# Expert products of a hybrid decoder step: a store on another queue, another spread of row chunks, an earlier load

## The reference, cut to what matters

```
ue = u[e]
ve = v[e]
a = jax.nn.gelu(jnp.einsum('nd,nhkd->nhk', xb, ue, preferred_element_type=f32), approximate=False)
return jnp.einsum('nhk,nhkd->nd', (g * a).astype(x.dtype), ve).astype(x.dtype)
```

## Time and profile before

| | |
|---|---|
| median of 3 runs | 2511.35 us (2506.83 to 2520.95) |
| the profiled execution | 2510.1 us, its span 2508.5 us |
| u part, first product to last | 955.5 to 1691.8 us |
| v part, first product to last | 1709.3 to 2393.9 us |
| TensorE busy, share of the span | 87% |
| VectorE busy | 54% |
| ScalarE busy | 14% |
| moved by DMA | 511.81 MB, mean 204 GB/s |

### The profile page before, as it was taken

One profiled execution on the slowest core, in us unless ns is written; L12 is line 12 of the kernel. 1 busy time (PEld: TensorE's weight loads), 2 busy tenths in 40 slices (PEclk: granted clock), 3 DMA queues, 4 the chain that ended last, 5 costly groups with the idle time before them and its releaser, 6 DMA issues. The chain is left out here.

```text
span 2508.5 us, 24546 instructions
## 1 busy us (share of the span) xinstructions
PE 2177.9 (87%) x8879; PEld 1609.9 (64%) x8879; DVE 1360.6 (54%) x2817; ACT 358.3 (14%) x743; POOL 338.3 (13%) x316
## 2 busy tenths in 40 slices
PE   7968899869999899999987888887787788789997
PEld 4745687637889566777654666665555555457776
DVE  2006577644441796999854777774544555451022
ACT  1001276420101012111100122220000000000011
POOL 1011000030000002222222111112222222210000
PEclk9979999875599899999998999998989999889999
DMA  3241121131223326999888777769999999976521
GB/s 117 51 91 64 43 101 51 28 108 51 111 81 101 108 94 258 337 346 346 307 315 291 268 257 287 265 236 355 335 324 324 338 330 328 334 264 209 180 82 45
DMA packets 181423, 511.81 MB, mean 204 GB/s; under 512 B 16589, under 2 KB 103253, under 8 KB 154038
## 3 DMA queue, kind: packets, MB, share of 16 engines
q1 hardware_dynamic: 146358, 294.72, 35.1%
q0 software_dynamic: 31488, 213.94, 22.5%
q10 hardware_dynamic: 3456, 1.57, 0.2%
HBM read 460.45 MB, written 49.72 MB: 203 GB/s over the span
## 5 line engine op out<-in xcount | busy, mean ns | idle before, releaser
L1878 PE MATMUL ex_ps<-proj,ex_ring 128*128 128x320 f32 x2048 | 585.7, 449 | 116.6 <-DVE proj L2037 99.0
L1823 PE MATMUL ex_ps<-h,ex_ring 128*128 128x320 f32 x2048 | 583.4, 446 | 34.7 <-DMA ex_ring<-in_uT 24.1
L1878 PEld LDWEIGHTS ex_ps<-proj,ex_ring 128*128 128x128 f32 x2048 | 404.0, 198 | 298.0 <-issue 129.9
L1823 PEld LDWEIGHTS ex_ps<-h,ex_ring 128*128 128x128 f32 x2048 | 398.7, 197 | 202.7 <-DMA ex_ring<-in_uT 28.1
L1967 DVE CUSTOM_DVE_ANT_0 proj<-proj,gx_tokens 128x1024 f32<-128x1024 f32 x120 | 145.8, 1222 | 208.5 <-DMA proj<-in_uv,at_upper 106.8
L1742 POOL DMA_INDIRECT proj<-in_uv,at_last x76 | 108.2, 1424 | 403.0 <-DVE gx_sum L1984 390.4
L1984 DVE SCALAR_TENSOR_TENSOR gx_sum<-proj,gx_sum 128x1024 f32<-128x1024 f32 x120 | 154.2, 1285 | 4.3
L1912 ACT ACTIVATE proj<-proj 128x2 f32<-128x2 f32 x100 | 20.2, 203 | 764.7 <-DVE proj L1967 764.7
L1854 PE MATMUL ex_ps<-attT 128*128 128x128 f32 x640 | 90.5, 295 | 42.6 <-DVE attT L1961 42.6
L379 PE MATMUL gate_ps<-h,work 128*128 128x260 f32 x512 | 120.2, 389 | 3.1 <-DMA work<-in_w_t 3.1
L1854 PEld LDWEIGHTS ex_ps<-attT 128*128 128x128 f32 x640 | 85.1, 206 | 54.6 <-DVE attT L1961 44.1
(11 more groups left out here) (361 smaller groups left out, 2607.0 us busy)
## 6 DMA issues: line engine op xcount, KB each, us to landing
ex_ring<-in_uT SPq DMA_DIRECT2D x128, 512.0 KB, 4.9
ex_ring<-in_uv SPq DMA_DIRECT2D x128, 512.0 KB, 5.9
scratch_a<-ex_gelu SPq DMA_DIRECT2D x128, 160.0 KB, 4.1
scratch_w<-proj SPq DMA_DIRECT2D x10, 2048.0 KB, 7.4
proj<-scratch_a SPq DMA_DIRECT2D x32, 640.0 KB, 7.5
proj<-scratch_w SPq DMA_DIRECT2D x32, 640.0 KB, 11.2
work<-in_w_t SPq DMA_DIRECT2D x37, 512.0 KB, 3.6
mg_ring<-in_w_q SPq DMA_DIRECT2D x32, 512.0 KB, 3.4
```

The costliest lines, as they stand in the source:

```text
L1823: last = nc.tensor.matmul(y[:, bank(n), 0:TD], u[:, n % UR, k, :], xn[:, k, 0:TD], start=(k == 0), stop=(k == DC - 1))
L1878: last = nc.tensor.matmul(y[:, m, 0:TD], ring[:, (E1 + e) % UR, m * P:(m + 1) * P], H[e // EG % 2][:, e % EG, :], start=(e == 0), stop=(e ...
```

## The change

Four edits, all in `experts`. The store of the gelus leaves SP's queue and is issued by ScalarE behind each gelu, with a wait for that gelu. SP's wait for the gelu goes with it. The load of the gate weights of group `g + 2` stands behind the first tile of group `g`, not behind the last one and the load of the gelus. The 48 chunks of the v part are spread over all 32 groups, one behind even groups and two behind odd ones.

```diff
@@ SP, u part
                 if n + UR < E1:
                     sp.wait_ge(s_pu, n + 1)
                     load_u(n + UR)
-                sp.wait_ge(s_ge, n + 1)
-                sp.dma_start(A_dram[n], ge[:, n % UR, :]).then_inc(s_as[n % UR], 16)
...
@@ SP, v part
                 g = e // EG
+                if e % EG == 0 and g + 2 < NE:
+                    sp.wait_ge(s_h, (g + 1) * EG)
+                    load_weights(g + 2)
                 if e % EG == EG - 1 and g + 2 < NE:
                     load_hidden(g + 2)
-                    sp.wait_ge(s_h, (g + 1) * EG)
-                    load_weights(g + 2)
@@ ScalarE, gelu(n)
                 nc.scalar.activation(ge[:, n % UR, :], y[:, bank(n), 0:TD], ACT.Gelu).then_inc(s_ge, 1)
+                act.wait_ge(s_ge, n + 1)
+                act.dma_start(A_dram[n], ge[:, n % UR, :]).then_inc(s_as[n % UR], 16)
@@ VectorE, behind the gating of group g
-                for _ in range(V_CHUNKS):
+                while chunk < U_CHUNKS + (NC - U_CHUNKS) * (g + 1) // NE:
                     chunk_of(chunk)
                     chunk += 1
-            assert chunk >= NC
```

More of the change, by code:

```diff
@@ L1657, in experts @@
     U_CHUNKS = PRE_CHUNKS + NG // W_EVERY
-    V_CHUNKS = 2
     def tile_at(us):
```

## The result

The change takes 2384.92 us (median of 4 runs, 2374.52 to 2387.90) against 2509.68: a ratio of 0.949, with a 95% interval of 0.945 to 0.953. The prediction was 2451 with 2421 to 2487 as its range. So the direction was right and the gain twice what was forecast: 125 us, not 60.

A forecast was written before the change was run, and what follows sets the result against it. The prediction took gathered bytes through a busy DMA to bound the v part's first half. Even chunks -60, sooner gate loads 0 and the store 0 took the profiled 2510.1 us to 2450, as a median 2451 us, range 2421 to 2487.

The forecast's parts named there:

- The bound before: V part, groups 0 to 23: VectorE late from two chunks ahead of each gating, gathered bytes through a busy DMA fixed.
- Even chunks: V part: chunks spread 1.5 a group over 32 groups, products ending at 2334 instead of 2394, -60 us.
- three limits of a group: V part, per group: TensorE 17.5 us, VectorE 17.3, DMA 18.4 to 19.7, the DMA's being the largest.
- second rival: V part: TensorE becomes the bound, 32 x 17.5 = 560 us, needing 368 GB/s; kernel 2387 us; chance 0.05.
- The end of the v part: Last two chunks behind group 31's gating: done about 32 us after group 29, TensorE needs 35; cost zero.
- Uneven pairs: V part: alternating one- and two-chunk groups idle TensorE and cost clock; 2488 us if gelus land at 12 us; chance 0.18.
- Sooner gate loads: V part: earlier gate-weight loads gain nothing by themselves, only cover for the even chunks; counted at 0.
- The store at 0, between -33 and +10: U part before tile 88: store moved to ScalarE's queue; TensorE's gain is waited out at tile 88; 0 us.
- the stalls of the u part go too: Rival, before tile 88: earlier tile loads leave gathers an emptier DMA, -60 - 30, 2421 us; chance 0.07.
- The bytes up to tile 88 are the same: U part: the prediction's argument against the rival in which the u part's stalls go too.
- The store's price: ScalarE, 128 tiles: wait and issue 0.35 us each, 45 us, taken as covered; up to 4 us if not.
- a third queue: U part, 25 tiles between 1240 and 1391: ScalarE's DMA row takes from gathers, 0.25 us a store, +6 us.

The follow-up runs named there:

- the last run: Changed kernel with add ahead of dot before tile 88 and in the v part, old order between the gate weights: 2337.20 us, 0.933 of the kernel before.

## Why the prediction was wrong by a half

*The bound before.* That VectorE was late because of the two chunks ahead of the next gating was right: the spread alone (93 us) and the order of add and dot alone (92 us) each took most of it away. The sentence behind it, that "the fixed quantity in the first half is gathered bytes through a busy DMA", was wrong. A share of 0.91 and 327 GB/s looked like a limit; they were what the chain asked for.

*Even chunks: the step that failed.* Of the three limits of a group, TensorE's 17.5 measured 17.45 in the blocks without a gap, and VectorE's 17.3 was about right: it is early enough to wait for gelus ahead of 13 gatings, 28.4 us in all. The third, 206 MB at 327 to 347 GB/s, 18.4 to 19.7 us a group, was no limit: the change ran at 367. The upper end of the rate was taken from the 17 us in which no product ran, as if a busy stretch without TensorE showed all that the DMA can do. The trace of before had already shown more. These are the rates of its stretch 1709 to 2251 in forty slices of 13.55 us:

```profile
GB/s 345 340 345 381 378 259 355 329 321 319 335 359 307 346 277 286 338 340 372 286 328 384 286 347 390 287 321 343 349 295 335 381 277 337 333 361 291 309 302 221
```

A mean of 327 made of slices up to 390 is no sign of a top at 347. Put in TensorE's limit for the DMA's, and the prediction's own sum gives the 2387 of its second rival, to which it gave 0.05. That 2387 lies so near the 2384.92 is partly luck: the v part took 571 us where that rival had 560, and the store took 11 us off the u part, which it had at 0. That rival needed 368 GB/s, and 367 came; the page of the Trainium skill that was named beside it (DMA: Bandwidth & Descriptors, "Bandwidth") gives 425 for a core alone, and no run here, up to 403, contradicts it.

*The end of the v part.* The last add was forecast to cost nothing, and so it is: it ends at 2256.8, and TensorE's last product at 2268.9, while VectorE waits 12.7 us.

*Uneven pairs.* They are there, gatings going 13.0, 23.1, 14.8, 23.5 us apart from 1906 on:

```profile
1906.10 1.72 DVE L2037 TENSOR_TENSOR proj<-proj 128x320 f32<-128x320 f32 x4
...
1919.08 1.70 DVE L2037 TENSOR_TENSOR proj<-proj 128x320 f32<-128x320 f32 x4 [2.69 <-DMA proj<-scratch_a]
...
1942.22 1.72 DVE L2037 TENSOR_TENSOR proj<-proj 128x320 f32<-128x320 f32 x4
...
1957.05 1.72 DVE L2037 TENSOR_TENSOR proj<-proj 128x320 f32<-128x320 f32 x4
...
1980.55 1.72 DVE L2037 TENSOR_TENSOR proj<-proj 128x320 f32<-128x320 f32 x4
```

A long one is 6 us over TensorE's group. The prediction let a gating be 7.1 us ahead while gelus land in 8.7; they land in 8.5, and 11.2 us of waits are all that is left of it, 0.7 us a pair where 0.9 was forecast. So the working held for the idle time. The 2.2 us of clock a pair did not come: behind the wait of 3.65 us eight groups took 140.90 us, 17.6 each.

*Sooner gate loads at 0.* They brought 17 us of v part alone and 11 to 21 on top of even chunks. Their part as cover was seen (VectorE's 43.6 us of waits for gate weights in the even chunks alone, against 2.3 in the change); that they bring 17 us where VectorE had no wait for gate weights was not in the sum, and why they do stays open.

*The store at 0, between -33 and +10.* It brought 11 us. The reason given for 0, that TensorE's gain is waited out at tile 88, is what the trace shows: 31.26 us in one wait. What it missed is that VectorE's chunks themselves come sooner. The rival "the stalls of the u part go too" had that, in a larger size and by an emptier DMA just before tile 88, which is true of the smaller share only. When TensorE stops, at 1322, 6.7 us are already gained: the 32nd `dots_gelu` begins 367.5 us behind the first product, before 374.2. In the 106 us up to there the DMA was fuller than before, 338 GB/s against 310; what brought these 6.7 us stays open. The last four chunks add 2.8 (406.4, before 415.9). There the DMA is emptier: with TensorE stopped, 2 tiles are loaded from 1322 to 1362, where before 6 were from 1321 to 1371, and the gathers landed in 6.8 to 7.7 us, against 7.8 to 8.4. "The bytes up to tile 88 are the same" did not speak against it, since they were moved at another time.

*The store's price.* None, as taken. ScalarE issues in 326 ns (350 in the earlier trace rows):

```profile
1418.87 0.44 ACT L1898 ACTIVATE ex_gelu<-ex_ps 128x320 f32<-128x320 f32 x1 [3.62 <-PE ex_ps L1821]
1419.33 0.33 ACTq L1900 DMA_DIRECT2D scratch_a<-ex_gelu  x1
...
1427.97 0.33 ACTq L1900 DMA_DIRECT2D scratch_a<-ex_gelu  x1
1428.39 0.59 ACT L1907 COPY proj<-ex_ps 128x512 f32<-128x512 f32 x1 [0.45 <-PE ex_ps L1852]
```

The copy behind the issue still waits 0.45 us for TensorE, as in the earlier trace rows: the issue lies beside the product. VectorE's waits for ScalarE are 11.7 us in 8 over the whole span, before 11.8 in 8. The 6 us that the estimate from the Trainium skill (same page, "Queues, rings and completion order") would have added by a third queue are not seen in the sum, since the u part got shorter; no run shows them apart.

## What to carry to other kernels

A DMA that is 0.9 busy at a steady rate is not shown to be at its limit: before a sum is built on such a rate, ask which engine's order decides when the next transfer may start, and how many can be under way, and look at its rate in short slices, not only at the mean. In a ring, release a buffer before you wait for the next one, unless the step ahead of the release covers another engine's latency; the same two instructions were right in one order in two stretches of this kernel and in the other in the third. And work that was spread evenly under the engine that bounds gained twice here: the engine kept its pace, and the transfers found time that had stood empty.

## What the runs showed of the hardware

One core moved 367 GB/s over 542 us, 380 over 522 and 403 over 111 us, gathers of 8 KB rows among them, where 349 had been taken for the top; the DMA share reads up to 1.03 there, so 0.91 left room. The two queues' even shares of 45.6%, which the prediction took to agree with a rule of turns, were no rule of division either: in the change they are 56.5% and 44.0%, and before, counted in packets, the queues were not even, 57606 against 13104. And TensorE's granted clock in the v part was 0.91 with 21 waits of up to 8.6 us, 0.99 in the change with 5 of up to 3.6 us, and 1.00, its 2.4 GHz level throughout, in the last run with none between its products.
